# Masks added on TensorE, a query that carries minus the scale, and one scaling of the probabilities, in the sparse attention of a two-block network

## The reference, cut to what matters

```python
def masked_softmax(s, mask):
    s = jnp.where(mask, s, -jnp.inf)
    m = jnp.max(s, axis=-1, keepdims=True)
    m = jnp.where(jnp.isfinite(m), m, 0.0)
    e = jnp.where(mask, jnp.exp(s - m), 0.0)
    d = jnp.sum(e, axis=-1, keepdims=True)
    return e / jnp.where(d > 0, d, 1.0)
...
o = gb[..., 0:1] * o_cmp + gb[..., 1:2] * o_slc + gb[..., 2:3] * o_win
```

## Time and profile before

| | us |
|---|---|
| median of 3 runs (lowest, highest) | 3422.64 (3418.2, 3424.34) |
| the profiled execution's own time | 3421.85 |
| span of its trace | 3420.4 |
| TensorE, VectorE, ScalarE, GpSimd busy | 3195.9, 2247.0, 1299.3, 809.9 |
| mean granted TensorE clock | 0.964 of full |
| slots of the sparse attention | from 89.8 to 297.4 |

### The profile page before, as it was taken

One profiled execution on the slowest core, in us unless ns is written; L12 is line 12 of the kernel. 1 busy time (PEld: TensorE's weight loads), 2 busy tenths in 40 slices (PEclk: granted clock), 3 DMA queues, 4 the chain that ended last, 5 costly groups with the idle time before them and its releaser, 6 DMA issues. The chain is left out here.

```text
span 3420.4 us, 45197 instructions
## 1 busy us (share of the span) xinstructions
PE 3195.9 (93%) x17180; PEld 2716.7 (79%) x17180; DVE 2247.0 (66%) x4390; ACT 1299.3 (38%) x2284; POOL 809.9 (24%) x760
## 2 busy tenths in 40 slices
PE   7899989999999999997998989878989999999998
PEld 6456558888777788885776868768989999999998
DVE  4675556455556564645553347898778888888886
ACT  3343443223333432333452223327843434343433
POOL 1000430000100200023000013578824343424341
PEclk9889999999999999997999999989999999999999
DMA  4332112322211232221111222344699989998883
GB/s 141 138 128 82 44 44 93 105 87 90 84 56 56 74 101 96 98 94 54 58 41 58 96 74 92 105 162 175 230 328 315 317 314 316 313 313 312 309 314 116
DMA packets 180455, 515.19 MB, mean 151 GB/s; under 512 B 14992, under 2 KB 75408, under 8 KB 175120
## 3 DMA queue, kind: packets, MB, share of 16 engines
q1 hardware_dynamic: 128256, 305.70, 26.0%
q0 software_dynamic: 40464, 160.45, 13.8%
q10 hardware_dynamic: 11520, 46.15, 3.5%
HBM read 477.11 MB, written 35.13 MB: 150 GB/s over the span
## 5 line engine op out<-in xcount | busy, mean ns | idle before, releaser
L234 PE MATMUL bank<-h_hi,w_hi 128*128 128x512 f32 (+1 forms) x2528 | 967.9, 383 | 76.3 <-ACT w_hi L202 19.0
L234 PE MATMUL bank<-h_lo,w_hi 128*128 128x512 f32 (+1 forms) x2528 | 951.8, 376 | 0.0
L208 DVE TENSOR_TENSOR w_lo<-w_raw,w_hi 128x1024 fp32r<-128x1024 f32 (+1 forms) x468 | 599.1, 1280 | 309.8 <-ACT w_hi L202 306.2
L202 ACT ACTIVATE w_hi<-w_raw 128x1024 fp32r<-128x1024 f32 (+1 forms) x508 | 546.0, 1075 | 543.3 <-PE bank L234 528.9
L234 PEld LDWEIGHTS bank<-h_hi,w_hi 128*128 128x128 f32 x2528 | 486.6, 192 | 163.2 <-issue 51.6
L234 PE MATMUL bank<-h_hi,w_lo 128*128 128x512 f32 (+1 forms) x2528 | 597.6, 373 | 9.6 <-POOL w_lo L215 9.6
L234 PEld LDWEIGHTS bank<-h_lo,w_hi 128*128 128x128 f32 x2528 | 487.5, 193 | 65.9 <-issue 10.5
L234 PEld LDWEIGHTS bank<-h_hi,w_lo 128*128 128x128 f32 x2528 | 461.1, 190 | 75.5 <-POOL w_lo L215 10.2
L234 PE MATMUL bank<-e_hi,w_hi 128*128 128x384 f32 x1024 | 345.6, 338 | 5.9 <-DVE e_lo L2310 5.9
L234 PE MATMUL bank<-e_lo,w_hi 128*128 128x384 f32 x1024 | 344.3, 336 | 0.0
L2219 POOL DMA_INDIRECT own_row<-in_u_rows,own_e x128 | 154.9, 1210 | 324.9 <-DVE sums L2347 277.7
(11 more groups left out here) (419 smaller groups left out, 4610.4 us busy)
## 6 DMA issues: line engine op xcount, KB each, us to landing
w_raw<-in_w SPq DMA_DIRECT2D x476, 512.0 KB, 3.9
ada_w<-in_ada_w POOLq DMA_DIRECT2D x24, 1024.0 KB, 5.1
expert_weights<-G ACTq DMA_DIRECT2D x12, 2048.0 KB, 7.2
Gin<-expert_weights SPq DMA_DIRECT2D x32, 768.0 KB, 8.3
w_raw<-in_w SPq DMA_DIRECT2D x32, 704.0 KB, 4.0
hidden_ahead<-u_stage ACTq DMA_DIRECT2D x40, 192.0 KB, 3.1
ahead<-hidden_ahead SPq DMA_DIRECT2D x20, 384.0 KB, 6.3
na_bias<-in_bias ACTq DMA_DIRECT2D x4, 896.0 KB, 4.6
```

What stands on the lines that cost most here:

```text
L202: sc.activation(w_hi[s][:, 0:n], w_raw[raw_slot[u]][:, 0:n], ACT.Copy).then_inc(*w_hi_made.next(u))
L208: ve.tensor_tensor(w_lo[s][:, 0:n], w_raw[raw_slot[u]][:, 0:n], w_hi[s][:, 0:n], ALU.subtract).then_inc(*w_lo_made.next(u))
L234: m = te.matmul(out, wt, moving, start=(not low and k == 0 and moving is hi), stop=(low and k == len(blocks) - 1))
```

## The change

The masks' sign is turned (`far`, `cfar`: 0 or +1e30, float32r) by GpSimd at the start, beside a float32r copy of the identity; the masks are loaded into `q[1]` for that. The query is multiplied by -0.125 as it leaves PSUM (`turned_query`), so the scores in PSUM are minus the scaled ones. TensorE adds the mask: after both heads' scores, a matmul of the identity with `far` or `cfar` adds to each head's bank. VectorE takes the row minimum instead of mask, maximum and product (a guard stays in branch 0 of the first token tile), and ScalarE's exponential has scale -1 with that minimum as bias. The reciprocal and the gate are two scalars of one operation on the probabilities. Branch 0 is 32 keys wide, with a zero 32nd key that the mask hides.

```diff
--- before.py
+++ after.py
@@ -609,8 +609,10 @@
         tab = sb(st, "rope_tab", [P, 2 * T + 64 + P])
         cos, sin = tab[:, 0:T], tab[:, T:2 * T]
         cos_c, sin_c, perm = tab[:, 2 * T:2 * T + N_CMP], tab[:, 2 * T + 32:2 * T + 32 + N_CMP], tab[:, 2 * T + 64:]
-        neg = sb(st, "nsa_neg", [P, P])
-        cneg = sb(st, "cmp_neg", [P, TT, 32])
+
+        far = sb(st, "nsa_far", [P, P], F32R)
+        cfar = sb(st, "cmp_far", [P, TT, 32], F32R)
+        ident_r = sb(st, "nsa_ident", [P, P], F32R)
         gates = sb(st, "gates", [P, TT, 24])
         kc = sb(st, "kc", [P, 32])
         vc = sb(st, "vc", [32, P])
@@ -650,6 +652,10 @@
             ve.tensor_tensor(tb[:, 0:n], scratch, s, ALU.mult).then_inc(*dve.next("rope", name))
             ve.wait_ge(*dve.here())
             ve.tensor_tensor(dst, ta[:, 0:n], tb[:, 0:n], ALU.add).then_inc(*dve.next("roped", name))
+
+        def turned_query(u):
+
+            return ve.scalar_tensor_tensor(raw[:, :], lin[u % 2][:, :], -SCALE, ny[:, :], ALU.mult, ALU.mult)
 
 
 
@@ -700,8 +706,8 @@
 
         def first_scalar():
             sc.dma_start(tab[:, :], io["tabs"][:, TABS["cos"]:TABS["cos"] + 2 * T + 64 + P]).then_inc(*tab_in.next("in"))
-            sc.dma_start(neg[:, :], tabs("causal_neg", P)).then_inc(*neg_in.next("in"))
-            sc.dma_start(cneg[:, :, :], tabs("cmp_neg", TT * 32).rearrange("p (t c) -> p t c", t=TT)).then_inc(*cneg_in.next("in"))
+            sc.dma_start(q[1][:, 0:P], tabs("causal_neg", P)).then_inc(*neg_in.next("in"))
+            sc.dma_start(q[1][:, P:2 * P], tabs("cmp_neg", TT * 32)).then_inc(*cneg_in.next("in"))
             for n in range(2):
                 sc.dma_start(cw[n][:, :, :], io["cmp_w"][n]).then_inc(*cw_in[n].next("in"))
             split_hi(U["k_cmp"])
@@ -779,7 +785,7 @@
             split_lo(UQ[1])
             take_made("v_win")
             ve.wait_ge(*w_used.at(UQ[0]))
-            scaled(raw[:, :], lin[UQ[0] % 2][:, :]).then_inc(*dve.next("raw", 0))
+            turned_query(UQ[0]).then_inc(*dve.next("raw", 0))
             bank_of.taken(UQ[0], dve)
             ve.wait_ge(*dve.here())
             rope_vector(0, q[0][:, :], raw[:, :], T, cos, sin, t_bank[0][:, :])
@@ -830,13 +836,14 @@
         def place(g):
             m, b = divmod(g, 3)
             p, i = divmod(m, TT)
-            return m, b, p, i, (N_CMP if b == 0 else (i + 1) * P)
+            return m, b, p, i, (32 if b == 0 else (i + 1) * P)
 
         def tensor():
             query = None
             for g in range(slots + 3):
                 m, b, p, i, w = place(g)
                 if g == 0:
+                    te.wait_ge(*pool.at("masks"))
                     te.wait_ge(*dve.at("roped", "k_win"))
                     te.wait_ge(*dve.at("vc"))
                     te.wait_ge(*act.at("natural", 1))
@@ -850,7 +857,11 @@
                         if g:
                             te.wait_ge(*act.at("nsa exp", hh, g - 1))
                         key = (kc, keys[0], keys[1])[b]
-                        te.matmul(s_bank[hh][:, 0:w], q[p % 2][rows, i * P:(i + 1) * P], key[rows, 0:w], start=True, stop=True).then_inc(*pe.next("nsa scores", hh, g))
+                        te.matmul(s_bank[hh][:, 0:w], q[p % 2][rows, i * P:(i + 1) * P], key[rows, 0:w], start=True, stop=False)
+                for hh in range(2):
+                    if g < slots:
+                        part, mask = (s_bank[hh][:, 0:32], cfar[:, i, :]) if b == 0 else (s_bank[hh][:, i * P:(i + 1) * P], far[:, :])
+                        te.matmul(part, ident_r[:, :], mask, start=False, stop=True).then_inc(*pe.next("nsa scores", hh, g))
                 for hh in range(2):
                     if g >= 3:
                         m2, b2, p2, i2, w2 = place(g - 3)
@@ -901,7 +912,7 @@
                         sc.wait_ge(*dve.at("nsa max", hh, g))
                         if g >= 6:
                             sc.wait_ge(*pe.at("nsa turned", hh, g - 6))
-                        sc.activation(Pm[hh][m % 2][b][:, 0:w], s_bank[hh][:, 0:w], ACT.Exp, bias=small[hh][:, k + 1:k + 2], scale=SCALE,
+                        sc.activation(Pm[hh][m % 2][b][:, 0:w], s_bank[hh][:, 0:w], ACT.Exp, bias=small[hh][:, k + 1:k + 2], scale=-1.0,
                                       accum_out=small[hh][:, k + 2:k + 3]).then_inc(*act.next("nsa exp", hh, g))
                     if p < 3 and g % 12 == 1:
                         split_hi(UQ[p + 1] + 1)
@@ -911,8 +922,7 @@
                     sc.activation(o_hi[:, 4 + p2, :], o_banks[p2 % 2][:, :], ACT.Copy).then_inc(*act.next("nsa out", p2))
 
         def vector():
-            ve.wait_ge(*neg_in.at("in"))
-            ve.wait_ge(*cneg_in.at("in"))
+            ve.wait_ge(*pool.at("masks"))
             for g in range(slots + 3):
                 m, b, p, i, w = place(g)
                 if 0 < g <= slots and g % 2 == 0:
@@ -921,22 +931,29 @@
                     for hh in range(2):
                         S, sm, k = s_bank[hh], small[hh], 4 * b
                         ve.wait_ge(*pe.at("nsa scores", hh, g))
-                        part = S[:, 0:w] if b == 0 else S[:, i * P:(i + 1) * P]
-                        ve.tensor_tensor(part, part, cneg[:, i, 0:w] if b == 0 else neg[:, :], ALU.add).then_inc(*dve.next())
-                        ve.wait_ge(*dve.here())
-                        row_max(S[:, 0:w], sm[:, k:k + 1], sm[:, k + 1:k + 2], SCALE, b == 0).then_inc(*dve.next("nsa max", hh, g))
+                        least = ve.tensor_reduce(sm[:, k + 1:k + 2], S[:, 0:w], AX.X, ALU.min)
+                        if b == 0 and i == 0:
+                            least.then_inc(*dve.next())
+                            ve.wait_ge(*dve.here())
+                            least = ve.tensor_scalar(sm[:, k + 1:k + 2], sm[:, k + 1:k + 2], 1e20, None, ALU.min)
+                        least.then_inc(*dve.next("nsa max", hh, g))
                     for hh in range(2):
                         sm, k = small[hh], 4 * b
                         ve.wait_ge(*act.at("nsa exp", hh, g))
                         c = 3 * p + 12 * hh + b
-                        row_scale(Pm[hh][m % 2][b][:, 0:w], sm[:, k + 2:k + 3], sm[:, k + 3:k + 4], b == 0,
-                                  gates[:, i, c:c + 1]).then_inc(*dve.next("nsa probs", hh, g))
+                        if b == 0 and i == 0:
+                            ve.tensor_scalar(sm[:, k + 2:k + 3], sm[:, k + 2:k + 3], 1e-30, None, ALU.max).then_inc(*dve.next())
+                            ve.wait_ge(*dve.here())
+                        ve.reciprocal(sm[:, k + 3:k + 4], sm[:, k + 2:k + 3]).then_inc(*dve.next())
+                        ve.wait_ge(*dve.here())
+                        Pg = Pm[hh][m % 2][b][:, 0:w]
+                        ve.tensor_scalar(Pg, Pg, sm[:, k + 3:k + 4], gates[:, i, c:c + 1], ALU.mult, ALU.mult).then_inc(*dve.next("nsa probs", hh, g))
                     if p < 3 and g % 12 == 2:
                         split_lo(UQ[p + 1] + 1)
                     if p < 3 and g % 12 == 9:
                         ve.wait_ge(*w_used.at(UQ[p + 1]))
                         ve.wait_ge(*dve.here())
-                        scaled(raw[:, :], lin[UQ[p + 1] % 2][:, :]).then_inc(*dve.next("raw", p + 1))
+                        turned_query(UQ[p + 1]).then_inc(*dve.next("raw", p + 1))
                     if p < 3 and g % 12 == 10:
                         rope_vector(p + 1, q[(p + 1) % 2][:, :], raw[:, :], T, cos, sin, lin[UQ[p + 1] % 2][:, :])
                         bank_of.taken(UQ[p + 1], dve)
@@ -955,6 +972,13 @@
         def gpsimd():
             gp.wait_ge(*tab_in.at("in"))
             gp.tensor_tensor(none[:, :], cos[:, 0:256], cos[:, 0:256], ALU.subtract).then_inc(*pool.next("none"))
+            gp.memset(kc[:, N_CMP:32], 0.0).then_inc(*pool.next())
+            gp.wait_ge(*ident_in.at("in"))
+            gp.tensor_copy(ident_r[:, :], ident[:, :]).then_inc(*pool.next())
+            gp.wait_ge(*neg_in.at("in"))
+            gp.tensor_scalar(far[:, :], q[1][:, 0:P], -1.0, None, ALU.mult).then_inc(*pool.next())
+            gp.wait_ge(*cneg_in.at("in"))
+            gp.tensor_scalar(cfar[:, :, :], q[1][:, P:2 * P].rearrange("p (t c) -> p t c", t=TT), -1.0, None, ALU.mult).then_inc(*pool.next("masks"))
             after(gp, "nsa projections")
             for k in range(N_ADA // 2):
                 if k >= 2:
```

## The result

The changed kernel takes 3402.93 us in the median of 7 runs (3393.89 to 3408.88), the kernel before 3421.90 in 7 (3416.38 to 3425.78): a ratio of 0.9944, interval 0.9934 to 0.9953, or 19 us less. The forecast was 3404. The profiled execution took 3402.93 us, with a span of 3401.5.

What follows compares the result with a forecast made beforehand. The engine that ends last was taken to depend on the slot: VectorE at pair ends, TensorE in others. From 3421.85 us, -12.0 of work and -6.3 of clock gave 3403.6, say 3404, range 3394 to 3416.

Steps and rivals of the forecast that it cites:

- the forecast's own case: Whole kernel: 3404 us, itself 3398 to 3409, given a chance of 0.50.
- the first stretch: Six slots from 89.8 to 117.8 us: TensorE-bound at half clock, ten mask steps of 0.165, +1.6 us.
- The last pair's -4.8: Fourth head pair, no projection beside it: about 37.5 of 50 us, 6.7 left to the clock, 0.5 for friction.
- Rival 5: TensorE paces the whole stage, so VectorE's 64 us are worth nothing: slower, 3435 us; chance 0.08.
- the 0.487 of L599: VectorE's product with two scalars per partition: taken to cost the same as with one; upper end 0.69.
- 96 x 0.11 + 1.6 = 12.2 us at full clock: TensorE's added mask work: 96 identity loads and matmuls at 0.11 each, 1.6 for width changes at 32-wide transposes.
- A step there costs 0.165: One mask on TensorE in the first six slots at half clock: 0.11 us and a third of the result more.
- 3.6 + 3.7: TensorE's time for the two slots from 223.15 to 230.67 us after the change, from 4.05 + 3.47.
- The chain at the pair's end: From exponential to exponential in a pair's last wide slot: 6.0 us becomes 5.0.
- Half of 12.7: Five half-clock lapses after the first stretch, worth 12.7 us: half taken back, -6.3, ends 0 and -12.7.
- Rival 2: The clock stays full after the first stretch: all 12.7 us back, 3397.2 us; chance 0.15.
- 3 (none): Rival: the clock lapses stay or only move, -12.0 + 1 for dearer masks, 3411 us; chance 0.13.

Runs made afterwards that it cites:

- e7: Changed kernel plus 21 unread 128x512 matmuls, 7 ahead of the first scores and 14 ahead of the first ada matmul: 3390.79 us, 0.9903 of before.
- e10: Kernel before plus 21 unread 128x512 matmuls in TensorE's two gaps at the stage's start, nothing else: 3417.05 us, 0.9987 of before.
- e6: Changed kernel with the masks put back on VectorE, new scaling and minimum kept, branch 0 at 31 keys: 3402.47 us, 0.9938 of before.
- e9: Changed kernel with each mask matmul made twice: 3413.04 us, 0.9967 of before.
- e4: Changed kernel without the 96 mask matmuls, so nothing is masked: 3388.96 us, 0.9900 of before.
- e1: Kernel before with only the masks moved to TensorE; maximum, minus-scale product and gate product kept: 3410.30 us, 0.9963 of before.
- e5: Changed kernel with the old scaling of the probabilities (guard, gate product, one scalar) put back: 3408.25 us, 0.9955 of before.

## Why the prediction was right

*The time and its size.* 3404 against 3402.93, the forecast's own case. To be within 1.1 us is luck, since the 7 runs alone spread over 15. The work came to -12.7 (predicted -12.0) and the clock to -7.1 (predicted -6.3) in the table above. With the first stretch's 4.1 put to half clock altogether, as e7 and e10 have it, they are -14.6 and -5.2, so the terms were less near than the table shows. The sum was nearer than its terms: the first stretch lost 4.1 where 1.6 was put down, and the second and the last pair made it good. The last pair's -4.8 does not even follow from its own terms: 37.5 of 50 is 12.5 off, not 12, and 12.5 less 6.7 and 0.5 is 5.3; measured are 4.2.

*What bounds it.* That TensorE does wait, for VectorE, was the reading that mattered. Most of those waits are gone (11.3 us of TensorE's idle time before, 3.2 now), and TensorE is left with 6.5 us idle. Rival 5 took the high share of TensorE at its word, and falls. But its picture is true of the changed kernel: there, giving VectorE its mask work back (e6) changes nothing that can be told, and of 0.115 us on TensorE nearly all counts (e9, and e4 outside slots 30 and 34).

*VectorE.* The removed lengths were put at 57 us, with 7 of handoffs, and VectorE at 97 busy. By its groups, lengths fell from 169.7 to 114.2, 55.5: 57.2 removed as written, 5.7 back for the second scalar, and 4.0 off at the minimum. Of these 4.0, 0.5 is that it is shorter than the maximum (0.682 for 0.692 at 512); the rest is that the two heads' minima now stand back to back and overlap (two at 512 in 1.28). Yet the busy time in the windows fell only 49, to 105.5. Two things failed here: the second scalar was put at nothing, and a sum of lengths was taken from a busy time. The latter counts an overlap once, and 15 us of the groups overlapped before, 8.7 after. The two-scalar operation at "the 0.487 of L599" was 0.06 too cheap; the upper end, 0.69, was further off.

*The masks on TensorE.* "96 x 0.11 + 1.6 = 12.2 us at full clock": the step is there in three views (0.12, 0.115, and 0.23 a slot), and 96 of it are 11; e4's stage gives 9.3, as in some slots VectorE hides it, and e4's median 14. The 1.6 for one more change of width in branch 0 is not there: slot 33 pays 0.24 like the wide ones. The choice of the middle between 6 and 24 by the nearest rows held; the reason given for the 6, that a pass streams half as much, no row or run shows. "A step there costs 0.165" at half clock failed: it is 0.22, twice the other; the third holds for a mixed slot, not for a step of TensorE alone. At that step the ten masks counted for the first stretch are 2.2, not 1.6, and six slots hold twelve. That the mask step reaches 0.2, one of the signs of being wrong, is so at half clock alone.

*The first stretch* lost more to a thing that the prediction held fixed: half clock ended at 120.4, not 115.4. e7, which takes the half clock away, gains 11.3 in these slots. Why it ended 5 us later in the changed kernel is open.

*The slots.* 3.6 + 3.7 was 3.27 + 3.70; 3.65 + 1.95 was 3.38 + 1.83; 5.3 + 3.5 was 5.43 + 3.72. The narrow ones were judged 0.1 to 0.3 too dear, but for the 3.7, the wide ones 0.1 and 0.2 too cheap, and the six came to -2.9 for -2.6. The chain at the pair's end is 5.35 us, not 5.0: the sum there of minimum and exponentials left out ScalarE's copies, which now stand before the first exponential. That ScalarE is "late next" is shown in this one place only. The thin stretch is 3.7 us (141.9 to 145.56), 3.5 predicted; the wait for L828 is 0.82 of the 1.32.

*The clock.* Half of 12.7 was taken back after the first stretch; measured are 9.3 there, with the lapses at 146, 276 and 286 gone, and those at 197 and 249 (10.2 us each) now 6.8 us at 192 and 3.4 at 240. Rival 2 (all back) and 3 (none) were both near enough for the range, which the 7 runs' own spread of 15 us nearly fills by itself. The first stretch gave at least 2.2 of it away again, a side that the prediction did not give the clock.

*The signs named in advance.* The last score group at 272.1 us (274 to 280 given, so a little earlier than that), TensorE's waits for VectorE at some 7 (2.9, 1.6, 1.6 and 1.3 in its larger entries, weight loads included; under 10 given), slot 3.70 (3.7 given), fewer lapses after 140 (10.2 us at half clock for 37), and no later stage longer by as much as this one is shorter. Waits on the exponential did not take the place of those on VectorE: the weight loads' fell from 14.4 to 11.7 us, the matmuls' from 5.4 to none.

## What to carry to other kernels

Moving work from a late engine to the one that is nearly the pace pays only until the late one is no longer late: here each of three cuts was worth 10 to 15 us alone and all together 19, and the one that loads TensorE was worth nothing as the third. Equal slots at the same clock tell such parts apart where whole runs, with their lapses, don't. Try the cuts that put nothing elsewhere first, and price the moved one against a kernel that already has them. Where a stage starts with a long run at half clock beside a wait for a transfer, a few matmuls into a bank that nobody reads may be worth trying (12 us here beside the loop's 19, but 4 on the kernel before); judge them by the whole kernel's runs, not by the stage.

## What the runs showed that was not expected

- A second scalar per partition costs VectorE a fixed 0.06 us (0.487 to 0.546 at 512 elements, 0.241 to 0.301 at 31 and 32).
- A load and matmul of 128 rows and columns behind others of the same shape is a step of 0.115 us at full clock and 0.22 at half, less than one such load's own record lasts (0.19 and 0.29).
- The same kernel's runs spread by up to 20 us (e1, e9) with its clock lapses; in e1 a mean granted clock of 0.969 or 0.961 over a run tells which, though one run of e5 breaks the rule.
- Half clock cost about a third of the time spent in it in slots and in the rest (0.28 to 0.37), and a half only in a run of like steps on TensorE.
- In the six slots minimum and scaling add up, masks and minimum replace each other.
- 21 unread matmuls, 5.6 us of TensorE, took 12 us off the changed kernel and 4 off the one before.
- The rest of the kernel, the same instructions in all versions, took from 3118 to 3133 us in the profiled executions.
